# Twenty gate tiles of a projection done as ten two-by-two block products, seven half-size products in place of eight

## The reference

```
h = rms_norm(x, attn_norm)                      # 512 x 1024
proj = h @ w_in                                 # q, k, v, ..., g: the last 3*1024 columns are the gates
y_a, y_b, y_c = three branches of 512 features each, every one times its own w_proj (512 x 1024)
gates = sigmoid(g + b_gate)                     # three of 512 x 1024
mixed = gates[0]*y_a + gates[1]*y_b + gates[2]*y_c
x = x + mixed @ w_out
h = rms_norm(x); x = x + (silu(a)*b) @ w_down   # a, b from h @ w_gate_up
return rms_norm(x)
```

## Time and profile before

| what | value |
|---|---|
| median of 3 runs | 804.53 us (804.43 to 804.9) |
| the profiled execution | 805.06 us, of which the span from first to last instruction is 802.9 us |
| PE busy | 786.8 us, 98% of the span |
| weight loads (PEld) | 653.8 us, 81% |
| DVE busy | 492.1 us, 61% |
| ACT busy | 324.2 us, 40% |
| HBM read | 78.67 MB, 101 GB/s over the span |
| granted TensorE clock | 0.998 of full |

### The profile page before, as it was taken

The page is one execution under the profiler, slowest core; times in us unless marked ns, Lnnn a source line. Parts: engine busy times, 40 slices in busy tenths (PEclk is TensorE's granted clock), DMA queues, the critical chain, the costliest instruction groups (busy, mean ns, idle before and its releaser), DMA issues.

```text
span 802.9 us, 10900 instructions
## 1 busy us (share of the span) xinstructions
PE 786.8 (98%) x3571; PEld 653.8 (81%) x3571; DVE 492.1 (61%) x741; ACT 324.2 (40%) x520; POOL 20.9 (3%) x43
## 2 busy tenths in 40 slices
PE   5999999999999999999999999999999999999996
PEld 4878888888888888888888888888888888888885
DVE  7878686868643334443435455454555555799997
ACT  7265555556423323222224532222222223466554
POOL 4011010100000000000000000000000000000001
PEclk9999999999999999999999999999999999999999
DMA  7423231323233333323232233333233333353432
GB/s 224 118 78 96 54 103 53 100 58 87 70 105 105 105 96 87 104 78 108 102 105 79 80 90 94 105 105 100 83 104 105 91 91 105 107 193 121 145 106 105
DMA packets 128670, 81.18 MB, mean 101 GB/s; under 512 B 5420, under 2 KB 118116, under 8 KB 128644
## 3 DMA queue, kind: packets, MB, share of 16 engines
q1 hardware_dynamic: 128132, 80.79, 34.2%
q0 software_dynamic: 512, 0.07, 0.1%
HBM read 78.67 MB, written 2.10 MB: 101 GB/s over the span
## 4 chain that ended last, share of the span: by engine, by line
PE 97%; DVE 1%; issue 1%; DMA 0%; ACT 0%; POOLq 0%; POOL 0%; ACTq 0%; SPq 0%; DVEq 0%
PE bank L600 24%; PE bank L602 24%; PE bank L604 24%; PE bank L859 4%; PE bank L860 4%; PE bank L861 4%; PE bank L777 2%; PE bank L779 2%; PE bank L781 2%; PE bank L714 1%; PE bank L631 1%; PE bank L694 1%; PE bank L739 1%; PE bank L692 1%; PE bank L737 1%
## 5 line engine op out<-in xcount | busy, mean ns | idle before, releaser
L600 PE MATMUL bank<-operands,whi 128*128 128x512 f32 x864 | 338.4, 392 | 0.9 <-DVE operands L1295 0.9
L604 PE MATMUL bank<-operands,wlo 128*128 128x512 f32 x864 | 336.7, 390 | 0.0
L602 PE MATMUL bank<-operands,whi 128*128 128x512 f32 x864 | 336.5, 389 | 0.0
L1286 DVE TENSOR_TENSOR wlo<-raw,whi 128x1024 fp32r<-128x1024 f32 x116 | 141.9, 1224 | 140.3 <-ACT whi L921 137.5
L600 PEld LDWEIGHTS bank<-operands,whi 128*128 128x128 f32 x864 | 162.3, 188 | 35.0 <-issue 1.3
L604 PEld LDWEIGHTS bank<-operands,wlo 128*128 128x128 f32 x864 | 162.2, 188 | 33.8
L602 PEld LDWEIGHTS bank<-operands,whi 128*128 128x128 f32 x864 | 162.3, 188 | 33.3 <-issue 0.2
L921 ACT CAST whi<-raw 128x1024 fp32r<-128x1024 f32 x116 | 121.1, 1044 | 76.2 <-PE bank L604 53.9
L927 ACT ACTIVATE work<-work 128x512 f32<-128x512 f32 (+1 forms) x24 | 15.2, 632 | 82.3 <-DVE work L1626 80.2
L1068 ACT ACTIVATE work<-bank,vecs 128x512 f32<-128x512 f32 x24 | 16.5, 689 | 78.0 <-PE bank L604 78.0
L1525 DVE TENSOR_TENSOR work<-bank,work 128x512 f32<-128x512 f32 x24 | 15.8, 688 | 41.1 <-PE bank L604 29.6
(11 more groups left out here) (212 smaller groups left out, 827.8 us busy)
## 6 DMA issues: line engine op xcount, KB each, us to landing
raw<-in_w_in_dram SPq DMA_DIRECT2D x106, 256.0 KB, 3.2
raw<-in_w_gate_up_dram SPq DMA_DIRECT2D x88, 256.0 KB, 3.1
raw<-in_w_down_dram SPq DMA_DIRECT2D x55, 256.0 KB, 2.8
raw<-in_w_out_dram SPq DMA_DIRECT2D x16, 256.0 KB, 2.9
big_x<-in_x_dram SPq DMA_DIRECT2D x4, 512.0 KB, 3.7
raw<-in_w_proj_attn_dram SPq DMA_DIRECT2D x8, 256.0 KB, 3.0
raw<-in_w_proj_pool_dram SPq DMA_DIRECT2D x8, 256.0 KB, 3.2
raw<-in_w_proj_conv_dram SPq DMA_DIRECT2D x8, 256.0 KB, 3.0
```

Of the source, the lines that this page charges most:

```text
L600: nc.tensor.matmul(banks[b][:, 0:width], whi[:, s, w], op(hi + k * S), start=a, stop=False)
L602: nc.tensor.matmul(banks[b][:, 0:width], whi[:, s, w], op(lo + k * S), start=False, stop=False)
L604: mm = nc.tensor.matmul(banks[b][:, 0:width], wlo[:, s, w], op(hi + k * S), start=False, stop=z)
L1286: nc.vector.tensor_tensor(wlo[:, s, :], raw[:, s, :], whi[:, s, :].bitcast(F32), ALU.subtract).then_inc(w_lo, 1)
```

## The change

The stage mix is no longer a loop. Four gate tiles (branches 0 and 1, column blocks 0 and 1) and their four projections are made as before. The other 20 gate tiles are taken as ten pairs, in ten "rounds" written out one after the other; `ROUNDS` lists them. A round takes two neighbouring column blocks of one branch. The product of weights (2 column blocks x 2 halves of the 1024 features) with h (2 halves of features x 2 halves of the tokens) is a two-by-two block product, done with seven products in place of eight (the Strassen-Winograd form). Each of the seven has 128 columns of weights, 512 features and 256 tokens: 4 feature blocks x 3 passes = 12 matmuls of 128 x 256. Three of the seven weight blocks are raw ones (B11, B21, B22), four are sums (T1 to T4). With the two projections PRJ_A and PRJ_B, in third and eighth place, a round has nine parts:

```diff
+ROUNDS = [(0, 2)] + [(i, br) for i in range(1, 4) for br in range(3)]
+PER_ROUND = 9
+        B11, B21, PRJ_A, T2, T1, T3, B22, PRJ_B, T4 = range(PER_ROUND)
+        TRIO = ((0, 1, 2), (4, 5, 6))
+        YIELDS = (3, 7)
```

PE. Before, in each loop turn `whole(...)` six times and `project(...)` three times. Now, after four `whole` and two `project`:

```diff
+            def quarter(r, j, b, x, first):
+                pe.wait_ge(w_lo, weight_part(r, j) + 1)
+                to = banks[b][:, 0:TOK]
+                wh, wl = part_at(whi, r, j), part_at(wlo, r, j)
+                for k in range(4):
+                    w = slice(k * P, (k + 1) * P)
+                    xh, xl = x(k)
+                    nc.tensor.matmul(to, wh[:, w], xh, start=first and k == 0, stop=False,
+                                     skip_group_check=not first)
+                    nc.tensor.matmul(to, wh[:, w], xl, start=False, stop=False,
+                                     skip_group_check=not first)
+                    mm = nc.tensor.matmul(to, wl[:, w], xh, start=False, stop=k == 3,
+                                          skip_group_check=not first)
+                mm.then_inc(used, 1)
...
+            for r in range(len(ROUNDS)):
+                a, b, d = TRIO[r % 2]
...
+                quarter(r, B11, a, rows_of(0, 0), True)
+                quarter(r, B21, b, rows_of(4, 0), True)
+                project_part(r, PRJ_A, 0)
+                if r == 0:
+                    pe.wait_ge(sums_lo_done, 4)
+                pe.wait_ge(kept, 3 * r + 1)
+                quarter(r, T2, a, sums_of(SUM2), False)
+                quarter(r, T1, d, sums_of(SUM1), True)
+                pe.wait_ge(kept, 3 * r + 2)
+                quarter(r, T3, a, sums_of(SUM3), False)
+                pe.wait_ge(posted, 4 * r + 1)
+                quarter(r, B22, b, sums_of(SUM4), True)
+                project_part(r, PRJ_B, 1)
+                pe.wait_ge(kept, 3 * r + 3)
+                quarter(r, T4, a, rows_of(4, 1), False)
```

```diff
+            for r in range(len(ROUNDS)):
+                last = r == len(ROUNDS) - 1
+                if r > 0:
+                    post(r - 1)
+                part_lo(r, T3, raw_part(r, 1, 0, 2), 2)
+                c11(r)
+                part_lo(r, PRJ_B, raw_part(r, 2, 1))
+                if r > 0 and ROUNDS[r - 1][1] == 2:
+                    merged_lo(r - 1)
...
+                part_lo(r, T4, weight_sum(2))
...
+                if not last:
+                    sum_weights(r + 1)
+                c12_first(r)
+                if 0 < r and not last:
+                    part_lo(r + 1, B11, raw_part(r + 1, 0, 0, 2), 2)
...
+                c22(r)
+                c12_second(r)
...
+                    part_lo(r + 1, PRJ_A, raw_part(r + 1, 2, 0))
+                    part_lo(r + 1, T2, weight_sum(1))
+                    part_lo(r + 1, T1, weight_sum(0))
```

ACT, in a round: the sigmoid of the previous round's last quarter, `keep` of B11, `whi` of T3 and B22, of PRJ_B, `first_gate`, (after branch 2: two `hi` of the merged blocks), `keep` of T2, `whi` of T4, `whi` of the next B11 and B21, `keep` of T3, `whi` of the next PRJ_A, T2 and T1 with `second_gates` before the last. A keep and its wait:

```diff
+            def keep(r, j, m, half):
+                act.wait_ge(used, weight_part(r, j) + 1)
+                nc.scalar.copy(work[:, at:at + TOK], banks[TRIO[r % 2][0]][:, 0:TOK]
+                               ).then_inc(kept, 1)
```

SP. A round loads three units into the three slots (gate columns of both column blocks, the two projections), each once the `lo` of the last part that lay in its slot is made. Since `big_x` has been overwritten, x is loaded again for the stage out:

```diff
+                if r == 0:
+                    sp.wait_ge(w_lo, PARTS_AT - 2)
+                else:
+                    sp.wait_ge(w_lo, weight_part(r - 1, B21) + 1)
+                    sp.wait_ge(weight_summed, 4 * r)
+                load_round(r, 0, gate_columns(br, 2 * i))
+                sp.wait_ge(w_lo, PARTS_AT - 1 if r == 0 else weight_part(r - 1, B22) + 1)
+                load_round(r, 1, gate_columns(br, 2 * i + 1))
+                sp.wait_ge(w_lo, PARTS_AT if r == 0 else weight_part(r - 1, PRJ_B) + 1)
+                load_round(r, 2, projections((br, 2 * i), (br, 2 * i + 1)))
...
             for j in range(8):
+                if j == SLOTS + 1:
+                    sp.wait_ge(used, weight_part(len(ROUNDS) - 1, B22) + 1)
+                    for t in range(TB):
+                        sp.dma_start(big_x[:, t * D:(t + 1) * D], x[t * P:(t + 1) * P, :]
+                                     ).then_inc(x_again, 16)
                 load_rows("out", 0, j, w_out, j % 4 * 2 * P, j // 4)
...
             def x1_half(c):
+                dve.wait_ge(x_again, 16 * TB)
```

More of the change, by code:

```diff
@@ L301, in hybrid_block @@
         RSTD, DIAG = big_y[:, 0:S], big_y[:, S:2 * S]
-        HALF = D // 2
         TW = 2 * P
@@ L396, in load @@
                 n, s = unit(stage, i, j)
-                if not (stage == "front" and n < SLOTS):
+                if stage == "out" and j < SLOTS:
+                    sp.wait_ge(w_lo, weight_part(len(ROUNDS) - 1, (B21, B22, PRJ_B)[j]) + 1)
+                    if j == 0:
+                        sp.wait_ge(weight_summed, 4 * len(ROUNDS))
+                    sp.sem_inc(loads_begun, 1)
+                elif not (stage == "front" and n < SLOTS):
                     sp.wait_ge(w_lo, n - SLOTS + 1)
@@ L448, in _ @@
                     load("pair", i, j, columns(w_in, i * P + col))
[L450 to L467, removed]
@@ L469, in _, with gate_columns, projections @@
-            for j in range(8):
+            def gate_columns(br, block):
+                return columns(w_in, COL_G + br * D + block * P)
+            def projections(first, second):
+                return [(w_proj[br][:, block * P:(block + 1) * P], at)
+                        for (br, block), at in ((first, 0), (second, WB))]
+            load("mix", 0, 0, gate_columns(0, 0))
+            load("mix", 0, 1, gate_columns(1, 0))
+            load("mix", 0, 2, projections((0, 0), (1, 0)))
+            load("mix", 0, 3, gate_columns(0, 1))
@@ L741, in _, with project @@
                     mm.then_inc(full[b], 1)
[L744 to L764, removed]
+            def project(j, parts):
+                s = unit_ready("mix", 0, j)
+                for half, (br, b, k) in enumerate(parts):
+                    begin(b, "mix", 0, k)
+                    mm = product(b, s, [(half * WB + c, c) for c in range(WB)], *BR[br],
+                                 True, True)
+                mm.then_inc(used, 1)
@@ L918, in split_hi @@
                 act.wait_ge(landed[s], 32 * loads_before(stage, i, j))
-                if not (stage == "front" and n < SLOTS):
+                if stage == "out" and j < SLOTS:
+                    act.wait_ge(used, weight_part(len(ROUNDS) - 1, (T1, B22, T4)[j]) + 1)
+                elif not (stage == "front" and n < SLOTS):
                     act.wait_ge(used, n - SLOTS + 1)
@@ new lines, in gate, with chunk_hi @@
+            def gate(j, b, to, br, block):
+                wait_unit(act, "mix", 0, j)
+                nc.scalar.activation(wk(to), banks[b][:], ACT.Sigmoid, bias=gate_bias(br, block)
+                                     ).then_inc(free[b], 1)
+            def chunk_hi(c):
+                act.wait_ge(sums_done, c + 1)
+                for n in range(2):
+                    nc.scalar.copy(sums_hi[:, (2 * c + n) * D:(2 * c + n + 1) * D],
+                                   tail_32[:, n * D:(n + 1) * D]).then_inc(sums_hi_done, 1)
@@ new lines, in merged_hi @@
+            def merged_hi(r, m):
+                act.wait_ge(merged, merged_by(r) + 1 + m)
+                operand_hi(op(MX_HI + (2 * ROUNDS[r][0] + m) * S), wk(ACC + m))
+            wait_full(act, 3, "pair", 3, 5)
+            act.wait_ge(vector_tile, count("vector_tile", "pair", 3, 1))
+            gate(0, 0, 0, 0, 0)
+            split_hi("mix", 0, 3)
+            split_hi("mix", 0, 4)
+            gate(1, 1, 1, 1, 0)
+            chunk_hi(0)
+            split_hi("mix", 0, 5)
+            gate(3, 2, 2, 0, 1)
```

412 lines of the change are left out of this document (343 added, 69 removed).

## The result

The changed kernel takes 797.47 us (median of 4 runs, 797.29 to 797.66) where the kernel before takes 804.57 us beside it: a ratio of 0.9911, 95% interval 0.9894 to 0.9928. That is 7.1 us less, 0.9%. Run again twice it took 797.96 us against 805.36 (ratio 0.9904, 0.9889 to 0.9919) and 797.39 us against 804.69 (0.9903, 0.9888 to 0.9918): 7.4 and 7.3 us less. 796.5 us was forecast, in a range of 795.5 to 799.5. Faster is shown; 8.0 us was forecast and 7.1 to 7.4 measured, and what follows asks where the rest is.

A forecast was written before the change was run, and what follows sets the result against it. PE's own work alone was taken to bound the mix stage: ten pairs saving 0.80 us each, other engines, transfers, opening and end costing nothing, so 804.53 - 8.0 = 796.5 us, range 795.5 to 799.5 us.

The forecast's parts named there:

- The bound: Mix stage: PE is busy for 195.87 of 195.87 us, so only PE's own work counts.
- 0.120 us for a half-width matmul: Assumed spacing of 128 x 256 matmuls in the rounds, from eleven steps at the trace's end; saves 0.80 us a pair.
- the other price, 0.1175: Alternative spacing in us of half-width matmuls, from four steps in the attention; would save 10.1 us over ten pairs.
- A round of 15.52 us: Forecast PE time of one mix round, where its share of the old loop was 16.32 us.
- the projections are the same work: Projections in the rounds stay 24 matmuls of 128 x 512, 5.44 us a round, as before.
- The walk: Edge-by-edge timing of one fullest round: everything PE waits on is ready 0.7 to 5 us early, costing nothing.
- the smallest one: Margin of 0.7 us: ACT's copy of T2 ends at 7.8 us in the round, PE wants it for T3 at 8.48.
- DVE's 84%: Forecast share of a round that DVE is busy, 13.1 of 15.52 us, where it was 41%.
- DVE as rival: DVE becomes the bound of the rounds; with 3 us more, 17.3 us a round and 814.5 us; chance 0.06.
- a cycle of 14.3 us: DVE's own time for the fullest round without its wait for PE from 7.2 to 8.4 us.
- The opening and the end of mix: Sums of h beside the first six units, and x reloaded before out: margins suffice, so both cost nothing.
- 95 GB/s: Transfer rate for weight blocks in mix, claimed to stay as it was before the change.

## Why the prediction was right, and what was off

- **The bound.** Right: PE alone. Eight products cost 1.44 us a round more, two idle DVE adds cost nothing.
- **0.120 us for a half-width matmul.** Right, over all 840, and the other price, 0.1175, was rounding. The formula of the Trainium skill (TensorE: Matmul & The Clock Gate, "Wait — 56ns, not 53.3ns?") would have given, as an estimate, 0.109 and a gain of 11.9 us; these traces do not agree with it (0.120 and 7.6 us in mix).
- **A round of 15.52 us.** Measured 15.56. The term "the projections are the same work" was mis-sized: each of them costs 2.75 us behind half-width matmuls, not 2.72. Net of the 0.01 us that the stretches beside it print less, that is 0.02 us for each of twenty, 0.4 us, and 8.0 became 7.6.
- **The walk.** Right within 0.3 us at every point compared; the margins it named are there. Moving T1 showed that the smallest one is load-bearing: without that cover 7.1 us are gone, all of the gain. One number beside the walk was off: DVE's 84% summed durations that overlap, and 76% was measured.
- **DVE as rival.** It stayed away, with more room than I gave it. For the fullest round I had a cycle of 14.3 us, which would cost something from 1.2 us more on and make the kernel slower than before from 2.0 us more on. Measured, 1.3 us more cost nothing in any round, and 3.5 us more made rounds of 17.0 us and a slower kernel; where between them it turns was not tried.
- **The opening and the end of mix.** Cost nothing, as worked out: 32.66 us for six units, 6 x 5.44 = 32.64, and the out stage starts without a pause. The transfers of x were issued at 393.2 us, 2.5 us before out and not 3.8, and nothing waited for them. The bytes per unit of time did not stay at 95 GB/s (65 in the opening, 107 in the rounds); that cost nothing either.
- **What I did not look at.** The stage down, 290 us behind the change, is 0.3 to 1.0 us longer in the three traces of the changed kernel (112.0 to 112.6 against 111.6 and 111.7). With it 7.6 becomes 6.6 to 7.3, and 7.1 to 7.4 were measured; the tenths by which the stages ahead of mix scatter are not in this sum. The place is known: PE waits there for DVE, which is behind, and DVE waits longer than before for blocks of `w_down` (1.1 us in all in both traces of the kernel before, 1.0 to 1.3 in the four kernels with more matmuls in mix, 1.5 to 2.2 in the changed kernel's three). Why these land later in this program is open. The instructions of down are the same, the four kernels with more matmuls in mix do not show it (111.3 to 111.8), those with added DVE work or the moved T1 do (112.1, 112.2; one execution each), and putting the adds first did not take it away.

No version tried beats the changed kernel.

## What to carry to other kernels

A product form that trades operations for smaller matmuls is to be priced per matmul, from a row of that very width with its weight loads, and not by its count of operations: of the 13.6 us that one eighth would be, 6.0 us went into the shorter matmuls and the changes of width here. Before it can earn anything, every copy between two products that share a bank needs another product beside it; one uncovered turn between the matrix engine and ScalarE, 0.7 us, cost as much as a round saves. Walk one round edge by edge with durations from the trace: it came out within 0.3 us, and it says roughly how much more the helping engines can bear: here it was too careful, as two idle adds cost nothing. Add work to a helping engine and time the added work in the trace too; here it was a sixth shorter than assumed.

## What the runs showed of the hardware that I had not expected

- Matmuls with a weight load each: 0.2267 us at 512 columns, 0.120 at 256, 0.111 at 128. Half the width again saves 8%, not half.
- The first full-width matmuls after shorter ones are slower: 0.02 to 0.03 us over a projection behind half-width ones, 0.11 us behind quarter-width ones.
- A wait of PE costs more than its idle column says: 0.46 us idle before T3 made the round 0.72 us longer.
- A stage with the same instructions took 111.3 to 112.6 us in 12 traces of 9 programs, and 112.0 to 112.6 in three traces of one program. That the program ahead of it decides this is not shown.
